# A one-core hybrid attention step: output weights scanned in the projection, cached rows scanned ahead of the first rotary steps, first frame loads issued after the phase barrier

## The reference

```
z = rms_norm(x, norm_mix_g) @ w_in
qa, ka, va, qd, kd, vd = split(z);  qa, ka, qd, kd = rope(...)
a = sink_attention(qa, [cache, ka], [cache, va], window mask, sinks)
w = softmax(qd0 kd0) - lam * softmax(qd1 kd1)          # chunk-causal
d = rms_norm(w @ [cache, vd], subln_g) * (1 - lam_init)
h = x + concat(a, d) @ w_out
y = rms_norm(h + swiglu(rms_norm(h, norm_ffn_g)), final_norm_g)
```

## Time and profile before

| | us |
|---|---|
| median of 3 runs (lowest, highest) | 2798.19 (2796.16, 2804.93) |
| the profiled execution | 2798.96 |
| its span | 2797.1 |
| PE busy | 2640.8 (94%) |
| DVE busy | 1577.2 (56%) |
| ACT busy | 1132.3 (40%) |
| POOL busy | 442.6 (16%) |
| mean granted clock of TensorE | 0.978 |

### The profile page before, as it was taken

The page is one execution under the profiler, slowest core; times in us unless marked ns, Lnnn a source line. Parts: engine busy times, 40 slices in busy tenths (PEclk is TensorE's granted clock), DMA queues, the critical chain, the costliest instruction groups (busy, mean ns, idle before and its releaser), DMA issues.

```text
span 2797.1 us, 47955 instructions
## 1 busy us (share of the span) xinstructions
PE 2640.8 (94%) x19784; PEld 1638.8 (59%) x19784; DVE 1577.2 (56%) x3264; ACT 1132.3 (40%) x2088; POOL 442.6 (16%) x526
## 2 busy tenths in 40 slices
PE   3899999958999997799999999999999999999998
PEld 1566666636677775355556565656565655556564
DVE  8676777658887774556454535253535444453516
ACT  4466666647888887444321111111111201111113
POOL 1111111104766665000000000000000000000001
PEclk9899999978999999899999999999999999999999
DMA  4122111151210010422101010000101010101003
GB/s 183 47 67 87 62 58 65 46 120 35 39 32 9 24 39 20 176 84 91 46 16 46 1 46 17 30 31 16 33 14 38 9 46 1 46 1 46 1 9 124
DMA packets 111932, 132.88 MB, mean 48 GB/s; under 512 B 42594, under 2 KB 89058, under 8 KB 110690
## 3 DMA queue, kind: packets, MB, share of 16 engines
q1 hardware_dynamic: 111714, 129.82, 14.6%
HBM read 92.20 MB, written 34.84 MB: 45 GB/s over the span
## 4 chain that ended last, share of the span: by engine, by line
PE 57%; DVE 1%; DMA 1%; ACT 0%; issue 0%; POOL 0%; POOLq 0%; ACTq 0%
PE y_ps L2265 6%; PE y_ps L2266 6%; PE y_ps L2267 6%; PE hnT_ps L2252 6%; PE hnT_ps L2253 6%; PE hnT_ps L2254 6%; PE mixT_ps L2252 6%; PE mixT_ps L2253 6%; PE mixT_ps L2254 6%; PE y_ps L2239 2%; PE y_ps L2238 2%; PE y_ps L2237 2%; PE mixT_ps L2212 1%; DMA tail_buffers<-mix_scratch 1%; PE hnT_ps L2222 0%
## 5 line engine op out<-in xcount | busy, mean ns | idle before, releaser
L2017 DVE SCALAR_TENSOR_TENSOR residual_rows<-y_ps,pair_scales,residual_rows 128x512 f32<-128x512 f32 (+1 forms) x374 | 276.9, 748 | 101.3 <-PE y_ps L2267 100.4
L2252 PE MATMUL hnT_ps<-ffn_inT_hi,tail_buffers 128*128 128x352 f16 x1056 | 330.7, 313 | 0.7 <-ACT ffn_inT_hi L2122 0.7
L2254 PE MATMUL hnT_ps<-ffn_inT_hi,tail_buffers 128*128 128x352 f16 x1056 | 330.8, 313 | 0.0
L2253 PE MATMUL hnT_ps<-ffn_inT_lo,tail_buffers 128*128 128x352 f16 x1056 | 330.7, 313 | 0.0
L2252 PE MATMUL mixT_ps<-ffn_inT_hi,tail_buffers 128*128 128x352 f16 x1056 | 330.1, 313 | 0.0
L2253 PE MATMUL mixT_ps<-ffn_inT_lo,tail_buffers 128*128 128x352 f16 x1056 | 330.0, 313 | 0.0
L2254 PE MATMUL mixT_ps<-ffn_inT_hi,tail_buffers 128*128 128x352 f16 x1056 | 330.0, 313 | 0.0
L2151 ACT ACTIVATE w_out_halves<-mixT_ps,pair_scales 128x352 f32<-128x352 f32 x66 | 36.6, 554 | 705.8 <-PE mixT_ps L2254 705.8
L1058 PE MATMUL z_ps<-w_in_hi_lo,normT_hi 128*128 128x384 f16 x816 | 268.7, 329 | 19.4 <-DVE w_in_hi_lo L654 19.4
L2265 PE MATMUL y_ps<-w_out_halves 128*128 128x512 f16 (+1 forms) x748 | 283.8, 379 | 0.0
L2005 DVE SCALAR_TENSOR_TENSOR w_out_halves<-hnT_ps,pair_scales,w_out_halves 128x352 f32<-128x352 f32 x66 | 38.5, 584 | 434.7 <-ACT w_out_halves L2151 434.7
(11 more groups left out here) (300 smaller groups left out, 5421.2 us busy)
## 6 DMA issues: line engine op xcount, KB each, us to landing
tail_buffers<-in_w_gate SPq DMA_DIRECT2D x11, 1024.0 KB, 5.1
tail_buffers<-in_w_up SPq DMA_DIRECT2D x11, 1024.0 KB, 7.5
tail_buffers<-in_w_down SPq DMA_DIRECT2D x22, 512.0 KB, 3.3
keys_values<-in_w_in SPq DMA_DIRECT2D x8, 1152.0 KB, 15.5
x_tile<-in_x SPq DMA_DIRECT2D x17, 512.0 KB, 3.6
tail_buffers<-mix_scratch SPq DMA_DIRECT2D x17, 512.0 KB, 3.7
residual_rows<-in_x SPq DMA_DIRECT2D x17, 512.0 KB, 4.5
out_y_prompt<-tail_buffers SPq DMA_DIRECT2D x16, 512.0 KB, 2.6
```

What stands on the lines that cost most here:

```text
L2017: nc.vector.scalar_tensor_tensor(out, YP[(2 * t + n) % 4][0:rows, :], PS[0:rows, i, F_YI:F_YI + 1], out, ALU.mult, ALU.add).then_inc(h_ok, 1)
L2252: nc.tensor.matmul(out, FH[w][:, k, c], nh, start=k == 0, stop=False)
L2253: nc.tensor.matmul(out, FH[w][:, k, c], nl, start=False, stop=False)
L2254: last = nc.tensor.matmul(out, FL[w][:, k, c], nh, start=False, stop=k == KC - 1)
```

## The change

- The scan of `w_out` moves from the last differential stage into the projection. SP issues two loads at the end of its iterations j = 5 to 8 into two free places of the frame keys' buffer; DVE reduces two pieces at the end of its iterations 6 to 9 (each now gives eight numbers per partition, of 128 instead of 256 elements), `w_out_max` follows in iteration 10, and POOL's all-reduce stands behind its last rotary add. The places are freed for keys from tile slot 11 on. The gains are loaded at the start of the program.
- At the start `cache_max` stands ahead of the first rotary step, POOL's second all-reduce directly behind its first, `score_scales` ahead of `norm_lo(1)`, and the splits of the cached rows and of tile 0's queries ahead of `xT_lo_out(1)`, on ACT likewise; PE runs `product(1, 1)` ahead of the turns of iteration 1 instead of behind them.
- The eight loads of stage 1's queries and one of its keys move from the end of the projection to the start of the differential phase, behind the meeting.
- The constant `dconsts` is made by three POOL instructions instead of one of DVE.

```diff
@@ phase_project, SP
+                def load_w_out(m):
+                    if m == 0:
+                        sp.wait_ge(x_lo, 3)
+                    else:
+                        sp.wait_ge(wo_scanned, m)
+                    for n in range(2):
+                        r = slice((m + n) * P, (m + n + 1) * P)
+                        sp.dma_start(WB[n], dram["w_out"][0, r, :].rearrange("p (a n) -> p a n", a=8)).then_inc(wo_in[n], 16)
...
                     if j == NTT + 1:
                         load_sample_values_lo()
-                        load_q(1, 0, (2, 3))
-                        sp.dma_start(K2D[0:HD, :, 0:4 * P], K1[0:HD, :, 0:4 * P]).then_inc(g.k2_in[1], 16)
...
-                    if j == NTT:
-                        load_q(1, 0, (0, 1))
...
+                        if WO_AT <= j < WO_AT + KC // 2:
+                            load_w_out(2 * (j - WO_AT))
@@ POOL
                 max_everywhere(0, S_MXW, S_AW)
+                max_everywhere(1, S_MXC, S_AC)
                 rotary_add(0, 0)
...
-                max_everywhere(1, S_MXC, S_AC)
...
+                pool.wait_ge(wo_local, 1)
+                nc.gpsimd.partition_all_reduce(g.ME[:, :], g.MA[:, :], P, RMAX).then_inc(wo_all, 1)
@@ DVE
+                def scan_w_out(m):
+                    for n in range(2):
+                        dve.wait_ge(wo_in[n], 16 * (m // 2 + 1))
+                        nc.vector.tensor_reduce(g.MO[:, 8 * (m + n):8 * (m + n) + 8].unsqueeze(2), WB[n], AX.X, ALU.max,
+                                                apply_absolute_value=True).then_inc(wo_scanned, 1)
...
                 weight_lo(1)
+                cache_max()
                 rotary(0, 0)
...
                 rotary(0, 2)
+                score_scales()
                 norm_lo(1)
                 weight_lo(4)
                 rotary(0, 3)
                 weight_lo(5)
-                xT_lo_out(1)
-                rotary(0, 4)
-                cache_max()
-                lambda_value()
-                score_scales()
                 cached_window_lo()
                 q_lo_window(0)
                 q_lo_diff(0)
+                xT_lo_out(1)
+                rotary(0, 4)
+                clear_holes()
+                lambda_value()
                 split_lo(0)
...
+                    if WO_AT < j <= WO_AT + KC // 2:
+                        scan_w_out(2 * (j - WO_AT - 1))
+                    if j == WO_AT + KC // 2 + 1:
+                        w_out_max()
@@ ACT
-                xT_hi_out(1)
-                values_out(0, 4)
-                values_out(0, 5)
                 act.wait_ge(scales_ok, 2)
                 act.wait_ge(init_ok, INIT)
                 cached_window_hi()
                 q_hi(0, 0)
                 q_hi(0, 1)
+                xT_hi_out(1)
+                values_out(0, 4)
+                values_out(0, 5)
@@ PE
                     if j == 1:
+                        product(j, 1)
                         pe.wait_ge(kc_lo, 1)
...
-                    if now:
+                    if now and j > 1:
                         product(j, 1)
@@ phase_differential, SP
+                load_q1(1)
+                load_ql(1)
+                sp.dma_start(K2[0:HD, :, 0:4 * P], K1[0:HD, :, 0:4 * P]).then_inc(k2_in[1], 16)
                 sp.dma_start(K2[0:HD, :, 4 * P:NT * P], K1[0:HD, :, 4 * P:NT * P]).then_inc(k2_in[2], 16)
@@ POOL
-                    if k == K - 6:
-                        pool.wait_ge(wo_local, 1)
-                        nc.gpsimd.partition_all_reduce(ME[:, :], MA[:, :], P, RMAX).then_inc(wo_all, 1)
```

More of the change, by code:

```diff
@@ L134 @@
 CACHED_AT = (2, 3, 4)
+WO_AT = 5
 XK_AT, CT_AT, XV_AT = 8, 11, 13
@@ L266, in phase_project @@
         w_in = [s(f"w_chunk_in{k}") for k in range(KC)]
+        wo_in = [s(f"w_out_in{n}") for n in range(2)]
+        gains_in, wo_scanned, wo_step, wo_local, wo_all = (
+            s(n) for n in ("gains_in", "w_out_scanned", "w_out_step", "w_out_max_local", "w_out_max_all"))
         small_in, rows_in, max_local, max_all, dve_step, scales_ok, wh_ok, wl_ok, lam_dot, lam_exp = (
@@ L355, in store_cached, with load_sample_q @@
                         sp.dma_start(g.xv[n], V[:, xv[0]]).then_inc(x_stored, 16)
[L357 to L363, removed]
+                def load_sample_q():
+                    sp.dma_start(Q1D[0][:, :, 0:P], g.q1[rows(0), :].rearrange("p (h n) -> p h n", n=P)).then_inc(g.q_in[0], 16)
+                    sp.dma_start(QLDF[0][:, 0, :, 0:HD], g.ql[rows(0), :].rearrange("p (h d) -> p h d", d=HD)).then_inc(g.ql_in[0], 16)
                 def load_sample():
@@ L403, in _ @@
                 load_cs(1)
+                sp.dma_start(g.SG[:, :], dram["subln_g"]).then_inc(gains_in, 16)
+                sp.dma_start(g.GF[:, :], dram["norm_ffn_g"]).then_inc(gains_in, 16)
                 for name in ("swa_k", "swa_v"):
@@ L646, in cached_lo, with w_out_max @@
                                                    col(S_A), vtile(VH, XV_AT + n)[:, :, 0:VD], ALU.mult, ALU.subtract).then_inc(x_lo, 1)
+                def scan_w_out(m):
[3 more added lines that the diff above has]
+                                                apply_absolute_value=True).then_inc(wo_scanned, 1)
+                def w_out_max():
+                    wo_link = Chain(dve, wo_step)
+                    dve.wait_ge(gains_in, 32)
+                    dve.wait_ge(wo_scanned, KC)
+                    wo_link(nc.vector.tensor_scalar(g.SG[:, :], g.SG[:, :], 1.0 - LAM_INIT, None, ALU.mult))
+                    wo_link(nc.vector.tensor_scalar(g.MO[:, 4 * KC:8 * KC], g.MO[:, 4 * KC:8 * KC], g.SG[:, :], None, ALU.mult))
+                    nc.vector.tensor_reduce(g.MA[:, 0:1], g.MO[:, :], AX.X, ALU.max, apply_absolute_value=True)
+                    nc.vector.tensor_reduce(g.MA[:, 1:2], g.GF[:, :], AX.X, ALU.max, apply_absolute_value=True).then_inc(wo_local, 1)
                 link = Chain(dve, dve_step)
@@ L888, in kT_out @@
                         act.wait_ge(x_stored, 48)
+                    if t == CT_AT:
+                        act.wait_ge(wo_scanned, KC)
                     nc.scalar.activation(K1[:, :, t * P:(t + 1) * P], TT[tb.bank["KD", j]][:, :].rearrange("p (h n) -> p h n", h=HC),
@@ L1370, in phase_differential @@
         CO = g.sb("dconsts", [P, 8], f32, ctx)
-        WB = [Q1[(len(plan.stage_first) - 2) % 2 ^ 1].rearrange("p h n -> p (h n)")[:, 2 * D * n:2 * D * (n + 1)].bitcast(f32) for n in range(2)]
-        SG, MA, ME, EX = (g.sb(n, [P, w], f32, ctx) for n, w in (("gain_sub", 1), ("max_parts", 2), ("max_everywhere", 2), ("exponents", 2)))
+        EX = g.sb("exponents", [P, 2], f32, ctx)
         TI = g.sb("tmp_int2", [P, 2], i32, ctx)
@@ L1437, in _ @@
                             load_ql(stage + 2)
-                        if stage == n_stages - 1:
-                            if h == 0:
-                                sp.wait_ge(s_ok, plan.stage_first[stage])
-                            for m in (2 * h, 2 * h + 1):
-                                if m > 1:
-                                    sp.wait_ge(wo_scanned, m - 1)
-                                sp.dma_start(WB[m % 2][:, :], w_out[m * P:(m + 1) * P, :]).then_inc(wo_in[m % 2], 16)
                         store(groups[4 * stage + h])
@@ L1450, in _ @@
             def _(pool):
+                nc.gpsimd.memset(CO[:, 1:2], EPS).then_inc(const_ok, 1)
+                nc.gpsimd.tensor_tensor(CO[:, 2:3], col(S_A), col(S_A), ALU.mult).then_inc(const_ok, 1)
+                pool.wait_ge(const_ok, 2)
+                nc.gpsimd.tensor_tensor(CO[:, 0:1], CO[:, 2:3], CO[:, 1:2], ALU.mult).then_inc(const_ok, 1)
                 pool.wait_ge(zero_ok, 5)
@@ L1594, in _ @@
                 maxima(groups[0])
-                dve.wait_ge(const_ok, 1)
                 dve.wait_ge(zero_ok, 5)
@@ L2307, in build @@
         g.GF, g.SO = g.sb("gain_ffn", [P, KC], f32), g.sb("gain_sub_scaled", [P, 1], f32)
-        g.MO = g.sb("w_out_max", [P, 4 * KC], f32)
+        g.SG, g.MO = g.sb("gain_sub", [P, 1], f32), g.sb("w_out_max", [P, 8 * KC], f32)
+        g.MA, g.ME = (g.sb(f"w_out_{n}", [P, 2], f32) for n in ("max_parts", "max_everywhere"))
         with ExitStack() as att:
```

37 lines of the change are left out of this document (9 added, 28 removed).

## The result

The changed kernel takes 2775.36 us, the median of 4 runs (2771.12 to 2775.86); the kernel before 2798.71 beside it (2796.16 to 2804.93). The ratio is 0.991, with a 95% interval of 0.9891 to 0.9929. The forecast was 2771.0 with a range of 2764 to 2782: the direction is right, the gain is 23.4 us instead of 27.9.

What follows compares the result with a forecast made beforehand. PE was taken to bound the kernel from the first row-max matmul to the meeting, with waits removable at three places: 2798.96 - 9.8 - 5.95 - 12.1 + 0 (scans) = 2771.1, stated as 2771.0 us, range 2764 to 2782.

Steps and rivals of the forecast that it cites:

- Start of the projection: Up to the first row-max matmul: it comes at 92.0 instead of 101.75 us, -9.8, bounds -5.5 and -12.
- the plain batch: At the start on DVE: weight_lo(2) runs without POOL's first add beside it, -0.73 us.
- the held add: POOL's first add falls into weight_lo(3), held to the batch's end: rotary(0,2) some 0.9 us late; other bound 0.
- the scale chain: score_scales, 3.5 us on DVE ahead of norm_lo(1), where DVE stood idle 1.71: +1.8 us.
- Rivals 2 and 5: Start-up gives half, DVE being late: 2775.4, chance 0.14; change fails at two of three places: about 2793, chance 0.03.
- rival 1: At the start, POOL's add is not held by the batch: 0.9 us better, 2770, chance 0.10.
- product(1,1) ahead of the turns: At the start on PE: its 24 matmuls, 4.0 us, run while ACT and DVE finish tile 0's splits.
- The meeting: Last store issued without the nine loads ahead; PE starts at 612.55 instead of 618.52: -5.95 us, bounds 0 to -6.5.
- rivals 4 and 6: Stage 1's loads land late, meeting's gain lost: 2777, chance 0.05; waiting for stage 1's queries makes it slower: chance 0.02.
- The scans: In the projection: 2.43 us of reduces in four DVE iterations, covered by 2.98 idle: 0, upper bound +4.4 us.
- rival 3: In the projection, scans delay the normalisation by 1.1 us in each of four tiles: 2775.4, chance 0.06.
- The end of the differential phase: PE's 10.77 us wait behind POOL goes; 54 matmuls run at full clock: -12.1 us, bounds -10.8 and -12.5.

Runs made afterwards that it cites:

- changed, second profile: The changed kernel run again with no edit: 2771.32 us, ratio 0.9904.
- before, two profiles: The kernel before, profiled first beside the changed kernel (2798.71 us), then once more with no edit (2796.28 us, one run).
- start-up alone: The kernel before with only the start-up reordering: 2790.12 us, ratio 0.9968.
- scans twice: The changed kernel with every scan of a piece of the output weights done twice, second result unused: 2775.78 us, ratio 0.9916.
- scan alone: The kernel before with only the scan of the output weights moved into the projection: 2788.82 us, ratio 0.9965.
- idle matmuls, both places: The changed kernel with four unused matmuls at the differential phase's start and thirteen in the projection's last iteration: 2774.43 us, ratio 0.991.
- loads alone: The kernel before with only stage 1's loads moved behind the meeting: 2793.28 us, ratio 0.998.
- changed, third profile: The changed kernel run a third time with no edit: 2771.86 us, ratio 0.9904.
- idle matmuls, stage only: The changed kernel with four unused matmuls in PE's waits at the start of the differential phase: 2772.82 us, ratio 0.9907.
- later scale: The changed kernel with POOL's second all-reduce behind its third rotary add, score_scales behind weight_lo(5), tile 1's turn copies earlier: 2772.64 us, ratio 0.9906.
- turns first: The changed kernel with product(1,1) back behind the turns of iteration 1: 2777.15 us, ratio 0.9921.
- loads undone: The changed kernel with stage 1's loads back in the projection, ahead of the last store: 2780.16 us, ratio 0.9931.

## Why the prediction was right, and where it was off

- **Start of the projection: right, by its own steps.** Forecast -9.8, measured -9.25. weight_lo(5) ends 3.9 us later (72.09 to 76.02) instead of 3.2: cache_max 1.47 (1.27), the plain batch -0.75 (-0.73), the held add 0.96 of idle time at 59.97 (0.9), the scale chain 2.2 (1.8). One step of the chain ran 0.72 us instead of 0.16, at the time of POOL's add of 61.60 (0.99). POOL's first add began at 55.81, the forecast 56.2, after 6.90 of code change. Rivals 2 and 5 fall with this and the next points.
- **What was luck in that gain.** The profile of the kernel before has the latest first row-max matmul of the four with the old start-up (101.75, against 101.13, 100.94 and 100.72); the eight profiles with the whole new start-up have 92.15 to 92.50. So the gain is 8.2 to 9.6, by the profiles that are set against each other, and the pair above lies near the upper end. And the forecast gave product(1,1) 4.0 us by the spacing of its last rows, while its first nine matmuls were 0.32 apart, at a granted clock of 0.50 (85.75 to 99.40 us); it had no reason for the full clock, which the changed kernel has there (1.00 from 75.75 to 92.50).
- **The choice between the two bounds of the held add: right.** It was held again, for 4.06 us, to 59.87, behind the end of its batch at 59.01. So rival 1, by which the hold lasts one DVE instruction, falls. The Trainium skill, "SBUF — State Buffer", section "Who interferes with whom", gives the shared ports for the whole instruction to whoever issues first, and says so of DVE in a two-port mode; the prediction carried it over to DVE instructions with two SBUF inputs. The trace does not agree with that reading: of the five POOL adds of the two traces that begin inside a batch, four took 4.06, 4.74, 5.00 and 6.20 us, and only the one at 48.25 took 1.29, while its batch took 5.06 instead of 4.31. What made that one different isn't shown.
- **product(1,1) ahead of the turns: right in sign, not in its reason.** The forecast has it run while ACT and DVE finish tile 0's splits. With the move undone the turns begin at 86.14 without a wait, so the splits are done by then; what the product covers is ACT's normalisation of tile 2, behind which the copies stand (the wait of 2.53). Undone, the move costs 2.6 us of the product's 4.0.
- **The meeting: right.** Pause 3.40 (forecast 3.7). The loads came in time: the list of PE's waits has none for them, and rivals 4 and 6 fall. `dconsts` on POOL came with 7.57 us of code change (7.5 forecast) and was done at 611.29, 8.5 us before POOL's next work; it was not tried alone.
- **The scans: right, cover and margin.** Alone the projection's stretch is 507.25 (507.10 and 506.93 in the two profiles of the kernel before), in the changed kernel 0.3 to 1.0 us longer by its three profiles; rival 3, with 4.4, falls, and the doubled scan shows that it would nearly have held with twice the work (3.3 to 3.8).
- **The end of the differential phase: right.** 4.17 us from the last score matmul instead of 16.63, -12.5 against -12.1.
- **The stretch between the meeting and that end: the step that failed.** The forecast took what PE gains at a wait to pass on in full through the work behind it, and counted the differential phase's own length as fixed. In its range it allowed 2 us for a higher clock behind the shorter pause, and nothing for a lower one. The length is not fixed. Summed over windows of 1 us, twice the share of the clock that is missing gives the time at half clock between the phase's first matmul and its last score matmul. In the profiles of this study it goes with the length:

| kernel | at half clock, us | length, us |
|---|---|---|
| changed, second profile | 33.6 | 486.27 |
| before, two profiles | 33.9, 33.9 | 486.48, 486.56 |
| start-up alone | 34.0 | 486.71 |
| scans twice | 39.3 | 487.38 |
| scan alone | 39.4 | 487.52 |
| idle matmuls, both places | 40.0 | 487.84 |
| loads alone | 40.1 | 487.91 |
| changed, third profile | 43.0 | 489.18 |
| idle matmuls, stage only | 43.0 | 489.17 |
| later scale | 43.3 | 489.44 |
| turns first | 43.6 | 489.25 |
| changed, first profile | 49.2 | 490.56 |
| loads undone | 49.2 | 490.48 |

The figures are not the time of the return alone. About 150 us into the phase the clock is at half once more, for 3.4 us in eleven profiles and for 6.8 in three (changed, third; idle matmuls, stage only; later scale), and with the turns first it is at half from 33.3 us after the first matmul for 10.2 us.

One more us at half clock costs 0.27 us (4.29 us of length over 15.6 between the changed kernel's own profiles). That it isn't more may be ACT, busy 14.25 of the 15.5 us in the windows at full clock; no run tests this. With the early return the changed kernel's execution took 2770.77 us, the forecast to 0.3; with the late one 2775.30. So the forecast was that of the early return, which it had not asked about; the three sets together, with a median of 2771.9, bear it out better than the first set did. The last phase took 1673.4 to 1678.8 us in the fourteen profiles, though no edit touches it; that it was equal in the first pair is luck too.

**What stays open:** what decides when the clock returns. It is not the code alone, since one kernel gave three answers, and not the loads. But it may not be chance alone either: three profiles of kernels with the old scan and the old loads have 34 us, and of eleven with either moved only one has. PE's pauses ahead of the phase (2.1 to 10.7 us) don't sort them. On the other side stand the mean granted clocks of whole executions. The kernel before has 0.974 to 0.979 in the 32 that ran beside the experiments, as wide a spread as the changed kernel's 0.979 to 0.984; the fourteen at 0.976 or below took 2798.1 to 2804.0 us, the ten at 0.978 or above 2794.9 to 2798.4. Its two profiles are at 0.978. So its executions lose different amounts of clock too, but no profile shows in which stretch. Whether the change makes a late return likelier, and so costs some of its own gain, isn't settled by three profiles on one side.

## What to carry to other kernels

The waits removed from the bounding engine passed on to the end of the stretch at all three places here, and a forecast by places, each with its own cover and bound, came within 0.6 us at each in the first pair of profiles. What it must not leave out is the clock of the stretch behind such a wait: where the rows show TensorE at half clock, the length of that stretch can differ between executions, here by 4.3 us, and a second profile of the same kernel tells how far it moves. One set of four executions was 3.5 us off the median of twelve. Work put into idle time of another engine should be tried at double size once: it shows how much cover is left.

## What the runs showed of the hardware that was not expected

- TensorE stayed at half clock while the rows show PE busy throughout: in the changed kernel from 611.53 us, the end of a wait, to 634.06 (22.53 of 22.53 us busy, granted clock 0.50), and after a wait of 0.63 us again to 649.2. In all fourteen profiles it first came back 30, 36 or 46 us after the phase's first matmul. With the turns first it came back after 29.9 us and was at 0.50 again from 639.8 to 649.8 us, PE busy for 10.00 of these 10.
- A POOL add that took 0.99 us at 61.60 (the same 128x384) took 6.20 us at 71.86: it was held not only to the end of the batch weight_lo(5) at 76.02 but through the splits that now follow it on DVE, and ran when DVE came to a wait at 77.20 (the idle 2.07 before 79.27). Here the elementwise work moved together on DVE lengthened the hold of POOL beyond the batch; in the kernel before the add at the same place took 5.00 us, to the end of the batch (67.95 to 72.95).
